# Expert weights in 512 KB halves, each with its own semaphore, at most three on their way

## The reference: what is computed

```python
logits = (xt @ router_w).astype(jnp.float32)
top_val, top_idx = lax.top_k(logits, TOP_K)               # TOP_K = 2
gates = jax.nn.softmax(top_val, axis=-1)
combine = jnp.einsum("nk,nke->ne", gates, jax.nn.one_hot(top_idx, N_EXPERTS))
for e in range(N_EXPERTS):                                # 8 experts
    y = y + combine[:, e:e + 1] * swiglu(xt, w_gate[e], w_up[e], w_down[e])
```

## Time and profile before

| | before |
|---|---|
| runs, median of 3 | 1658.75 us (1652.36 to 1661.92) |
| the profiled execution, its own time | 1652.49 us |
| its span, first to last instruction | 1650.3 us |
| TensorE matmul busy / weight load busy | 1525.6 us / 1323.6 us |
| moved by DMA | 433.39 MB |
| DMA in the experts' stage, 690 to 1590 us | 364 GB/s |
| transfer of a unit, issue to landing, same stretch | 7.1 us median |

### The profile page before, as it was taken

The page is one execution under the profiler, slowest core; times in us unless marked ns, Lnnn a source line. Parts: engine busy times, 40 slices in busy tenths (PEclk is TensorE's granted clock), DMA queues, the critical chain, the costliest instruction groups (busy, mean ns, idle before and its releaser), DMA issues.

```text
span 1650.3 us, 53537 instructions
## 1 busy us (share of the span) xinstructions
PE 1525.6 (92%) x25644; PEld 1323.6 (80%) x25644; DVE 261.4 (16%) x481; ACT 179.5 (11%) x389; POOL 141.1 (9%) x164
## 2 busy tenths in 40 slices
PE   7999999999999996998999899999998998998996
PEld 6786587777686754998888898898898998898896
DVE  3433310000243444000000000000000100100102
ACT  3233120000222324000000000000000000000001
POOL 1343200000032423000000000000000000000000
PEclk9999999999999997999999999999999999999999
DMA  9213244444421353799999999999999999999970
GB/s 307 101 52 128 102 165 152 152 152 139 185 83 70 129 204 153 295 382 363 347 354 370 358 375 376 350 378 377 360 362 358 367 362 370 349 350 371 359 271 27
DMA packets 147653, 433.39 MB, mean 263 GB/s; under 512 B 9050, under 2 KB 33884, under 8 KB 147436
## 3 DMA queue, kind: packets, MB, share of 16 engines
q1 hardware_dynamic: 146556, 427.75, 70.3%
q0 software_dynamic: 672, 2.14, 0.4%
q10 hardware_dynamic: 208, 0.08, 0.0%
HBM read 428.89 MB, written 1.05 MB: 261 GB/s over the span
## 4 chain that ended last, share of the span: by engine, by line
PE 90%; issue 5%; DVE 3%; ACT 1%; POOL 1%; SPq 0%; DMA 0%; DVEq 0%
PE ps L992 34%; PE ps L1012 17%; PE ps L880 9%; PE ps L589 8%; PE ps L891 4%; PE ps L752 3%; PE ps L600 3%; PE ps L1036 2%; PE ps L960 1%; PE ps L709 1%; PE ps L719 1%; PE ps L615 1%; PE ps L622 1%; PE ps L729 1%; PE ps L744 1%
## 5 line engine op out<-in xcount | busy, mean ns | idle before, releaser
L992 PE MATMUL ps<-wpost,ring 128*64 128x88 f32 x5376 | 217.3, 241 | 20.1 <-issue 19.1
L992 PE MATMUL ps<-AT_sb,ring 128*64 128x88 f32 x5376 | 214.4, 240 | 19.5 <-issue 19.4
L1012 PE MATMUL ps<-LT_sb,ring 128*64 128x88 f32 x5376 | 216.6, 240 | 16.9 <-issue 15.7
L992 PEld LDWEIGHTS ps<-wpost,ring 128*64 128x64 f32 x5376 | 210.0, 138 | 27.1 <-issue 26.4
L1012 PEld LDWEIGHTS ps<-LT_sb,ring 128*64 128x64 f32 x5376 | 208.6, 137 | 25.9 <-issue 24.5
L992 PEld LDWEIGHTS ps<-AT_sb,ring 128*64 128x64 f32 x5376 | 207.5, 137 | 26.6 <-issue 26.2
L880 PEld LDWEIGHTS ps<-hT_sb,ring 128*128 128x128 f32 x768 | 136.0, 190 | 24.6 <-issue 9.1
L880 PE MATMUL ps<-hT_sb,ring 128*128 128x256 f32 (+1 forms) x768 | 155.7, 362 | 0.0
L589 PE MATMUL ps<-hT_sb,ring 128*128 128x256 f32 x608 | 137.7, 385 | 0.0
L589 PEld LDWEIGHTS ps<-hT_sb,ring 128*128 128x128 f32 x608 | 116.0, 193 | 16.5 <-issue 0.5
L1702 DVE TENSOR_TENSOR LT_sb<-BM,ps 128x704 f32<-128x704 f32 (+1 forms) x32 | 25.5, 796 | 546.6 <-PE ps L992 546.6
(11 more groups left out here) (272 smaller groups left out, 1096.1 us busy)
## 6 DMA issues: line engine op xcount, KB each, us to landing
ring<-in_moe_w_gate SPq DMA_DIRECT2D x84, 1024.0 KB, 6.9
ring<-in_moe_w_up SPq DMA_DIRECT2D x84, 1024.0 KB, 7.3
ring<-in_moe_w_down SPq DMA_DIRECT2D x84, 1024.0 KB, 7.1
late<-in_moe_w_up SPq DMA_DIRECT2D x28, 1024.0 KB, 7.2
late<-in_moe_w_gate SPq DMA_DIRECT2D x28, 1024.0 KB, 7.1
late<-in_moe_w_down SPq DMA_DIRECT2D x28, 1024.0 KB, 7.4
ring<-in_ffn_w_gate SPq DMA_DIRECT2D x11, 1024.0 KB, 5.4
ring<-in_ffn_w_up SPq DMA_DIRECT2D x11, 1024.0 KB, 8.0
```

The source lines that it names most:

```text
L992: ins = mm(o[lo:lo + P // 2, :], w[:, i, m * P + lo:m * P + lo + P // 2], xgT[e % 2][:, k, :], start=(k == 0 and m % 4 == 0), stop=(k == K ...
L1012: ins = mm(o[lo:lo + P // 2, :], d[:, i, m * P + lo:m * P + lo + P // 2], moe_hid[:, 2 * j + i, :], start=(first and m % 4 == 0), stop=las ...
```

## The change

Each unit is issued as two transfers of 512 KB, the first half and the second half of its rows. Each half has its own semaphore, of which there are two sets of eight (N_SEM) in place of one set of sixteen. In the first round, before SP issues a half it also waits until the half three places ahead of it in the queue has landed, so that no more than three are on their way (IN_FLIGHT). TensorE waits for each half by itself, ahead of the first weight load that reads it. In a second or third round there is no limit of three, but unit n waits for unit n - 8. The buffers, the order of the units and all arithmetic are as before.

```diff
@@ -97,6 +97,9 @@
     LAST_UNIT[_u[:3]] = _n
 ROUND_UNITS = len(UNITS)
 assert ROUND_UNITS % N_UNIT == 0
+HALVES = 2
+IN_FLIGHT = 3
+N_SEM = 8
 N_STEPS = 25
 ROUTE_GD = 15
 LEVELS = 7
@@ -288,7 +291,7 @@
 
         ring_landed = [sem(f"ring_landed{i}") for i in range(NSLOT)]
         ring_used = sem("ring_used")
-        unit_landed = [sem(f"unit_landed{i}") for i in range(N_UNIT)]
+        unit_landed = [[sem(f"half{h}_landed{i}") for i in range(N_SEM)] for h in range(HALVES)]
         unit_used = sem("unit_used")
         x_landed = [sem(f"x_landed{t}") for t in range(TT)]
         consts_landed, rows_landed, heads_landed, router_landed = (
@@ -510,7 +513,7 @@
                     if first and n < N_UNIT:
                         first_free(n)
                     else:
-                        sp_.wait_ge(unit_used, per_round(r, n - N_UNIT + 1, ROUND_UNITS))
+                        sp_.wait_ge(unit_used, per_round(r, n - (N_UNIT if first else N_SEM) + 1, ROUND_UNITS))
                     if kind == "d":
                         lo = (MOE_AT[c] + 2 * j) * P
                         dst = down_unit(n)
@@ -521,7 +524,13 @@
                         dst = gate_unit(n, c)
                         src = (moe_gate if kind == "g" else moe_up)[0, e][ks.start * P:ks.stop * P, f]\
                             .rearrange("(k p) f -> p k f", p=P)
-                    sp_.dma_start(dst, src).then_inc(unit_landed[n % N_UNIT], 16)
+                    rows_at = dst.shape[1] // HALVES
+                    for i in range(HALVES):
+                        if first and n * HALVES + i >= IN_FLIGHT:
+                            m, hf = divmod(n * HALVES + i - IN_FLIGHT, HALVES)
+                            sp_.wait_ge(unit_landed[hf][m % N_SEM], 16 * (m // N_SEM + 1))
+                        part = slice(i * rows_at, (i + 1) * rows_at)
+                        sp_.dma_start(dst[:, part, :], src[:, part, :]).then_inc(unit_landed[i][n % N_SEM], 16)
 
             moe_loads(0, True)
             sp_.wait_ge(rounds_ready, 1)
@@ -970,8 +979,10 @@
                     ins = mm(bank(6)[0:SLOTS, t * P:(t + 1) * P], onehot[e % 2][:, t, :], ident_bf, start=True, stop=True)
                 ins.then_inc(ohT_ps, 1)
 
-            def landed(r, n):
-                pe.wait_ge(unit_landed[n % N_UNIT], per_round(r, 16 * (n // N_UNIT + 1), 16 * ROUND_UNITS // N_UNIT))
+            def landed(r, n, i, ni):
+                if i * HALVES % ni == 0:
+                    pe.wait_ge(unit_landed[i * HALVES // ni][n % N_SEM],
+                               per_round(r, 16 * (n // N_SEM + 1), 16 * ROUND_UNITS // N_SEM))
 
             def m_in(r, kind, e, c):
 
@@ -983,9 +994,9 @@
                 b = 0 if kind == "g" else 2
                 for j in range(MOE_TILES[c] // 2):
                     n = UNITS[kind, e, c, j]
-                    landed(r, n)
                     w = gate_unit(n, c)
                     for i, k in enumerate(gate_ks(c, j)):
+                        landed(r, n, i, len(gate_ks(c, j)))
                         for m in range(MOE_TILES[c]):
                             o = bank(b + m // 4)[:, m % 4 * SLOTS:(m % 4 + 1) * SLOTS]
                             for lo in (0, P // 2):
@@ -1002,9 +1013,9 @@
                     pe.wait_ge(yT_dve, per_round(r, e, N_EXP))
                 for j in range(MOE_TILES[c] // 2):
                     n = UNITS["d", e, c, j]
-                    landed(r, n)
                     d = down_unit(n)
                     for i in range(2):
+                        landed(r, n, i, 2)
                         first, last = c == 0 and j == 0 and i == 0, c == MOE_CH - 1 and j == MOE_TILES[c] // 2 - 1 and i == 1
                         for m in range(KD):
                             o = bank(4 + m // 4)[:, m % 4 * SLOTS:(m % 4 + 1) * SLOTS]
```

## The result

The change makes the kernel slower: 1802.32 us median (1794.2 to 1807.94, 4 runs) against 1660.34 us (1652.36 to 1662.68, 4 runs) of the kernel before beside it. The ratio is 1.0817, with a 95% interval of 1.0777 to 1.0856. I had forecast 1578 us in a range of 1556 to 1640.

The account below looks back on a forecast made before the run. It took PE, stopped by instruction fetches late behind weight transfers, as the bound. 82 us gained by supply less 5 for remaining stops took 1652.5 to 1575.5; half of 6.3 us on top gave 1578.5, range 1556 to 1640.

Parts of the forecast that it names:

- the 95 us: Experts' stage, 690 to 1590 us: time PE loses to stops for late instruction fetches, the most the change can win.
- (a): PE's stops in the experts' stage: at most three halves out shortens fetch delays, 90 of 95 us gone.
- Rival 3: PE's fetches: their delay does not go with the queue, the stops stay, 1652 to 1659 us; chance 0.08.
- (b): Weight supply under the limit: 2.6 to 3.1 us a unit, 2.75 taken; last expert matmul ends at 1551.5.
- The signs that I had named for this: Signs of supply misjudged: landings of 4.5 us and over, PE waiting for weights early, DMA under 350 GB/s.
- The formula for the end: Last unit lands at 672.7 plus 319 times the time per unit, 1550.0 at 2.75; PE needs 1.5 us more.
- The break-even of 3.01 us a unit: Weight supply: pace at which the last landing comes at 1632 and nothing is gained; 4.5 us per half.
- Rival 1: Weight loads: the limit starves the DMA engines, a half takes 5.0 us, kernel slower at 1755 us; chance 0.13.
- (c): SP's queue: one more instruction per unit and wait per half cost nothing while buffers are full, else under 0.1 us.
- (d): PE's 336 extra waits for halves: between 0 and 13 us, taken as 0.
- (e): Before 672 us: the limit on the first 16 units, landed when PE comes to them, costs 0 either way.
- rival 2: Weight supply in between, 2.85 to 3.0 us a unit, 50 to 2 us gained; chance 0.17.

Follow-up runs that it names:

- e9: The change (three halves out) with the second half of each unit never loaded, PE's work kept whole: 1558.42 us, one run.
- e1: The change with at most four halves on their way in place of three: 1643.79 us, ratio 0.9854 to the kernel before.
- e12: Four halves out run again, with more rounds and a second profile: 1643.61 us, ratio 0.9887 to the kernel before.
- e5: The change (three halves out) with an eighth of the experts' matmuls, the rest left out: 1767 us, one run.
- e4: The change with whole 1 MB units, at most two on their way, 16 semaphores: 1669.37 us, ratio 1.0008 to the kernel before.
- e3: The kernel before with each unit issued as two 512 KB transfers, no limit on how many are out: 1661.47 us, ratio 0.9973.
- e2: The change with at most six halves on their way in place of three: 1662.08 us, ratio 0.9965 to the kernel before.
- e6: The change with four halves out and an eighth of the experts' matmuls, the rest left out: 1557 us, one run.
- e7: The kernel before, whole units without a limit, with an eighth of the experts' matmuls: 1520 us, one run.
- e10: The change with two halves out and an eighth of the experts' matmuls, the rest left out: 2118 us, one run.
- e11: The change with one half out and an eighth of the experts' matmuls, the rest left out: 3047 us, one run.

## Why the prediction was wrong

- **What bounds the kernel before: right.** PE was held up by something that goes with the weights' traffic, not by late weights, and the 95 us for it agree with e9 (94 us against the profile before; 119 against the run beside it). That it is the instruction fetch is inferred from the period of 128 matmuls and the 16 KB packets; no view times a single fetch. The Trainium skill ("Runtime: NRT & Kernel Launch", Instruction fetch mechanics) calls that crossing "mostly hidden"; by this reading that does not hold beside a full stream of weights, and does at half the traffic (0.2 us of stops in e9).
- **(a), the stops go at three halves: right in the outcome, wrong in the rule.** They fell to 3.4 us, and from 675 to 800 us, with PE at full pace, from 11.9 to 1.7. But I had them shrink in proportion to the bytes out. At 2 MB out (e1, e12), 57 to 61 us of 69 to 79 are left. The table shows what they go with: while the engines' share is 0.96 to 0.98 the stops are 45 us or more; they are gone at 0.89 to 0.90 and at 0.69. That is not because PE, held up by transfers, asked for instructions more slowly: from 675 to 800 us and in e9 it wasn't held up. So the fetch was in time where the weights left the engines idle for a tenth of the time, and here that is also where the weights come too late. Share and bytes out fell together in these runs (1.5 MB at 0.89, 0.9 MB at 0.69), so a steep effect of the bytes between 1.5 and 2 MB is not ruled out.
- **Rival 3 is out as it was put.** It had the 95 us stay, and they went. Its mechanism is not out in full. The Trainium skill's rule ("DMA: Bandwidth & Descriptors", Queues, rings and completion order) has an engine take turns between its queues. A fetch that waits for a turn only where the engine is busy would also be late at a share of 0.98 and less often at 0.9; no run here tells that from a wait behind the backlog. My words that the stops are too long for one packet's turn rest on no row.
- **(b), what the limit does to the supply: wrong, and this is the step that failed.** I put "2.75, nearer to the lower end" for a unit. It was 3.49: 602 halves were issued from 690 to 1740 us, 1.744 us each. I had divided the 3.9 us of a half with nothing ahead of it by three. A half with two others out takes 5.0 to 5.1 us (e5 and the change), so 1.7 us each. PE first waited for a transfer at 815.9 us, and not in the last quarter of the stage. The two transfers of the earlier trace rows that landed 1.3 us apart were both issued before either had landed, and so were three more behind them, by 2.9 us. The second took 4.7: that row held the warning. The 1.0 us of a fetch, from which I built the upper end of 3.1, is not what it hangs on (5.0 against 5.1 us). The signs that I had named for this came: landings over 4.5 us, under 350 GB/s, PE waiting from early on.
- **The formula for the end: right.** Landing of the last unit at 672.7 + 319 r. With r = 3.49 it gives 1786.0, and 1787.5 with the 1.5 us behind it; the last expert matmul ended at 1788.7 (1787.25 + 1.43). The break-even of 3.01 us a unit agrees with e4: a unit of 1.049 MB at 350 GB/s is 3.00 us, and its ratio is 1.0008, though there a part of the time is still stops.
- **Rival 1 was the outcome.** It had L = 5.0 us for half the excess of a loaded unit and gave 1755; L was 5.1 and the time 1802 to 1808. By its own formula L = 5.1 gives 3.40 us a unit and 1778 us. Most of the rest, 28 us, is the difference to 3.49: three times 1.744 is 5.23 us from one issue to the third one after it, 0.1 us more than the median landing, and that counts on all 319 units. How much of it is SP's reaction, which (c) had inside the range of (b), and how much is that the mean landing is not the median, stays open. It got 0.13. What spoke for it (7.1 us under load against 4.9 alone) weighed more than I gave it: I took that excess for queueing which the limit would remove, but 5.1 - 3.6 = 1.5 us of it per half stays.
- **(c), (d), (e): no cost shown where supply is early.** e3 and e2 have the extra issues, and e2 the extra waits as well, at 0.9973 and 0.9965.
- **A slip in rival 2.** At 2.92 us a unit, 1604 to 1606 is when the last unit lands and is used. The kernel's time by the same formula is 1625 us, without any stops left.

Where the gain went: it was there, as the stretch from 675 to 800 us and e9 show, and from 816 us on it was more than paid back, with 166.4 us of PE's waits for transfers in the whole stage (128.1 of them from 690 to 1590 us).

## What to carry to other kernels

Latency of one transfer alone is not the latency of one in a window: measure or read it with as many out as the window has, and divide by that. A limit on what is in flight that has to hold the stream at 364 GB/s needed four halves here (2 MB); three gave 303. When an engine's "issue" stops come at a fixed count of instructions and vanish when the transfers end, suspect its instruction fetches. Half the bytes took the stops away here; fewer instructions were not tried; a limit just above what the supply needs won 1.1 to 1.5%. And look at the change before its buffers run empty: those 125 us showed the gain and the cost apart.

## What the runs showed of the hardware

- Time to landing of 512 KB (128 rows of 4 KB, or 2 x 2 KB), with one, two, three and four halves out and an eighth of the expert matmuls: 3.6, 4.4, 5.0, 5.2 us; rates 144, 235, 310, 389 GB/s; without a limit (1 MB transfers) 407. With all of the matmuls: 5.1 us and 303 GB/s at three, 5.7 us and 364 GB/s at four.
- 2 MB out as four halves gave 364 GB/s, as two units 350.
- With no limit on what is out, and with SP's loads waiting for PE, splitting each 1 MB transfer in two cost nothing (ratio 0.9973, interval 0.9945 to 1.0002).
- PE stood still for up to 2.5 us at a time, which I read as late instruction fetches, beside a DMA share of 0.96 and over. At full pace it had 1.7 us of such stops in 125 us at a share of 0.90 and 0.2 us in 800 at 0.69.
- TensorE's granted clock was 1.00 in the stretch of every kernel that kept it busy, 0.98 in the changed kernel, and 0.50 to 0.58 in e5, e6, e7, e10 and e11, where it was busy for 205 to 506 of 760 us. In the changed kernel transfers set the pace from 816 us on, and from 675 us to there the granted clock was 1.00.
